# Attentions of the first block: steps of four heads instead of two, one step deep, with four fixed score banks

## The chip, the cores and the metric

The kernel runs on one core of one Trainium2 chip (trn2). The metric is the device time of one execution in microseconds. Five engines have queues of their own, each worked strictly in order: TensorE (PE; PEld is its weight loads), VectorE (DVE), ScalarE (ACT), GpSimd (POOL) and SyncE (SP), which here only issues DMAs. They meet at semaphores: an instruction waits until a counter has reached a value. TensorE writes to PSUM, which has eight banks of 512 fp32 columns by 128 partitions.

## The reference

Two transformer blocks of two layers each, one after the other, on 256 tokens of width 1024, in fp32. The change touches the first block alone, and in it the two attention branches of each layer. In layer 0 the 256 context tokens attend to themselves (256 keys) and the 256 tokens of x attend to both (512 keys); in layer 1 only the tokens of x do (512 keys).

```python
q_m = (rms_norm(c_q, lw["mla_q_g"]) @ lw["w_uq"]).reshape(B, S, MLA_HEADS, MLA_QK_DIM)
q_nope, q_rope = jnp.split(q_m, [MLA_NOPE_DIM], axis=-1)     # 64 and 32 wide, 8 heads
...
y_m = attend(q_m, k_m, v_m) @ lw["w_mo"]                     # scores = nope part + rope part
...
y_g = attend(q_g, k_g, v_g) @ lw["w_go"]                     # 8 query heads, 2 key heads, 64 wide
g_f, g_m, g_g = jnp.split(jax.nn.sigmoid(gate_logits + lw["b_gate"]), N_BRANCHES, axis=-1)
return (g_f * y_f + g_m * y_m + g_g * y_g) @ lw["w_o"]
```

`attend` is scores, softmax over the keys, product with the values. `y_f` is a two-dimensional Fourier transform of four groups of 128 features, times `w_fo`. The key of the rope part is one for all eight heads.

## The kernel before

Every weight matrix streams through a ring of four slots of 1 MB ("panels"). SyncE asks for panel n when TensorE has begun panel n-3. There are two kinds. An "a" panel (`w_ada`, the modulation) is used as it lands. A "d" panel is split first: ScalarE rounds it to fp32r (`split`, L2050), GpSimd forms the rest (L1995), and TensorE multiplies three times (high by high and low, then low by high). The order of both kinds is the string `RING`.

The heads of the first block lie in pairs: pair c has head a = 0 in partitions 0 to 63 and head a = 1 in 64 to 127. The rope parts have 32 rows per head; the two of pair c lie in the strips that begin at 32 (c % 2) and at 64 + 32 (c % 2), with four copies of the one rope key, one per strip.

**The attention loop.** `units(l)` lists units (kind m or g, context or x, pair c, query tile q of 128 queries): 32 in layer 0, 16 in layer 1. Loop step u does on TensorE, in order:

- the scores of unit u: one product of 64 rows per head into a bank each, and for kind m one more of 32 rows per head (L1316 on);
- the transposes of the probabilities of unit u-2 (`TURN`), a bank per head, 2 or 4 tiles of 128 keys each;
- whatever of the other work is listed for u: `modulate()` (GROUPS, two "a" panels, each 16 products of 256 columns in column strips of 32, and the transposes of the modulation before), a Fourier step (`dft_steps`: products with `dft_d`, one step later with `cos_s` and `nsin_s`), `dense(2)` (OPENED, a gate panel), and the products with `w_fo` (FOURIER);
- the value products of unit u-3 (`LAG`): one bank per pair, both query tiles in it.

ScalarE in its step: the copies of the turned probabilities to SBUF (L2303), the two exponentials (L2319), the copy of a modulation row (L2066), the even half of a Fourier result (L2337), two sigmoids (L2348), a rounding of one group of the Fourier branch in four steps from ROUND (L2355), and splits of panels in the steps of AHEAD. VectorE: two row maxima (L3210) and their scaling (L3214), reciprocal and scaling of the probabilities of the unit before (L3220, L3224), the sum of a modulation (L2832), the copy of an attention output every second step (L3191), the Fourier halves (L3198, L3201, L3252 to L3255), and the low parts (L3264).

**Banks.** Every result takes the next of the eight banks in turn (`Tally.take`, the same count in every engine's program). Before TensorE writes to a bank it waits until the result before in that bank has been read (`bank()`). `T.last()` is the last bank taken. The steps in which the other work stands are written out by hand in GROUPS, LAST, OPENED, FOURIER, ROUND and AHEAD, one entry per layer.

Of the kernel before, what the change touches and what calls it, by code (L numbers as in the profile page):

```python
# [35 lines left out]
P = 128  # L36
# [149 lines left out]
RING = "a" * (ADA_FIRST - EARLY_ADA) + "d" * 10 + "a" * 16 + "dddd" + "a" * 10 + "d" * 50 \  # L186
# [4 lines left out]
class Tally:  # L191
# [3 lines left out]
    def __init__(self):  # L195
        self.count = {}
        self.regs = []
        self.bank = 0
# [14 lines left out]
    def take(self):  # L213

        b = self.bank
        self.bank = (b + 1) % BANKS
        return b, self.next(f"bank{b}")

# [8 lines left out]
    def last(self):  # L227

        b = (self.bank - 1) % BANKS
        return b, self.value(f"bank{b}")  # L230
# [231 lines left out]
def units(l):  # L462

    return [(kind, half, c, q) for kind in "mg" for half in ((0, 1) if l == 0 else (1,)) for c in range(HEADS // 2)
            for q in range(2)]
# [16 lines left out]
def pv_opens(u, todo):  # L482

    return LAG <= u < len(todo) + LAG and todo[u - LAG][3] == 0


def build(nc, W, out, scratch, copies):
    with ExitStack() as ctx:
# [11 lines left out]
        prob, probT = area(PROB, 2, 2, TOK), area(PROBT, 2, 4, SEQ)  # L500
# [91 lines left out]
        def _(sp):  # L592
# [142 lines left out]
            def mix_and_mlp(l):  # L735
# [16 lines left out]
                modulations(*((8, 16) if l == 0 else (36, 8)))  # L752
                for n in (0, 512):
                    gates(0, n)
                modulations(*((24, 10) if l == 0 else (44, 2)))
# [139 lines left out]
        def _(pe):  # L895
# [415 lines left out]
            def attention(l, cols):  # L1311
                todo = units(l)
                n = cols.stop - cols.start
                pv = first = None
                turned = {}
# [5 lines left out]

                dense(2)
                pe.wait_ge(S["roped"], T.next("roped"))
                for u in range(len(todo) + LAG):

                    if u < len(todo):
                        kind, half, c, q = todo[u]
                        keys = slice(0, HALVES[half][1])
                        c0 = HALVES[half][0] + q * P
                        qs = slice(c0, c0 + P)  # L1330
                        bs = [bank() for _ in range(2)]
                        for a in range(2):
                            at = slice(HD * a, HD * a + HD)
                            x, y = (qn[at, c, qs], kn[at, c, keys]) if kind == "m" else (qg[at, c, qs], kg[at, keys])
                            mm = products(ps[:, bs[a], 0:keys.stop], [(x, y)], stop=kind == "g")
                            if kind == "g":
                                mm.then_inc(k.bank_done[bs[a]], 1)
                        if kind == "m":
                            for a in range(2):
                                r0 = HD * a + ROPE * (c % 2)  # L1340
                                rot = slice(r0, r0 + ROPE)
                                products(ps[:, bs[a], 0:keys.stop], [(qr[rot, (2 * c + a) // 4, qs], kr[rot, keys])],
                                         start=False).then_inc(k.bank_done[bs[a]], 1)
                    if TURN <= u < len(todo) + TURN:
                        _, half, _, _ = todo[u - TURN]
                        pe.wait_ge(S["prob_ready"], T.next("prob_ready"))
                        for a in range(2):
                            b = bank()
                            for t in range(HALVES[half][1] // P):
                                mm = flip(ps[:, b, t * P:t * P + P], prob[:, (u - TURN) % 2, a, t * P:t * P + P])  # L1350
                            mm.then_inc(k.bank_done[b], 1)
                        turned[u - TURN] = T.last()

                    if u in GROUPS[l]:
                        modulate()
                    if u == LAST[l]:
                        modulated_last()
                    if u == 0:
                        fin_in = dense(1)
# [28 lines left out]
                    if u >= LAG:  # L1388
                        kind, half, c, q = todo[u - LAG]
                        tt = HALVES[half][1] // P  # L1390
                        if pv_opens(u, todo):
                            pv = bank()
                        pe.wait_ge(*k.moved(turned[u - LAG]))
                        for t in range(tt):
                            for a in range(2):
                                at = slice(HD * a, HD * a + HD)
                                h = 2 * c + a
                                mm = products(ps[at, pv, q * P:q * P + P],
                                              [(vm[:, t, h * HD:h * HD + HD] if kind == "m" else vg[:, t, at],
                                                probT[:, (u - LAG) % 2, t, a * P:a * P + P])], t == 0, t == tt - 1)  # L1400
                        if q == 1:
                            mm.then_inc(k.bank_done[pv], 1)
# [618 lines left out]
        def _(act):  # L2021
# [258 lines left out]
            def attention(l, cols):  # L2280
# [10 lines left out]

                fin_tiles((1, 2))
                turned = {}
                for u in range(len(todo) + LAG):
                    if u < len(todo):
                        tiles = [T.take() for _ in range(2)]
                    if TURN <= u < len(todo) + TURN:
                        turned[u - TURN] = [T.take() for _ in range(2)]
                    if LAG <= u:
                        tt = HALVES[todo[u - LAG][1]][1] // P  # L2300
                        for a, (b, v) in enumerate(turned[u - LAG]):
                            act.wait_ge(k.bank_done[b], v)
                            act.activation(probT[:, (u - LAG) % 2, 0:tt, a * P:a * P + P],  # L2303
                                           ps[:, b, 0:tt * P].rearrange("p (t c) -> p t c", t=tt),
                                           ACT.Copy).then_inc(k.bank_read[b], 1)
                    if u in AHEAD[l] and u not in OPENED[l]:
                        split()
                    if u < len(todo):
                        kind, half, c, q = todo[u]
                        buf = u % 2  # L2310
                        n = HALVES[half][1]
                        tt = 2 * half + q
                        if u >= TURN:
                            b, v = turned[u - TURN][1]
                            act.wait_ge(k.bank_done[b], v)
# [8 lines left out]
                    if u in GROUPS[l]:  # L2324
                        modulate()
# [1560 lines left out]
```

## Time and profile before

| | us |
|---|---|
| three runs | 2749.25, 2754.78, 2753.53 |
| median | 2753.53 |
| span of the profiled execution | 2752.9 |
| TensorE busy in it | 2696.1 (98%) |
| stretch of the attention of layer 0 (149.20 to 367.42) | 218.22 |
| stretch of the attention of layer 1 (1017.93 to 1138.58) | 120.65 |

The span runs from the first to the last instruction; the median of the runs is 0.6 us above it. A matmul's own duration contains its way through the array, so durations of neighbours overlap; the distance between the starts of two groups, best seen at the weight loads (PEld), is what the first of them costs. Idle time of an engine stands in brackets, with what ended it.

### The profile page before, as it was taken

The page shows a single profiled execution, that of the slowest core. Times are in us where ns is not written, and L with a number is a line of the kernel's source. Part 1 is how long each engine was busy: PE and PEld are TensorE (multiplying, and loading weights), DVE is VectorE, ACT ScalarE, POOL GpSimd, SP SyncE. Part 2 cuts the span into 40 slices and gives each one's busy share as a digit, 9 for nine tenths or more (in the row PEclk, how much of TensorE's full clock was granted, in tenths as well). Part 3 has the DMA queues.
Part 4 walks back from the last instruction along what each step waited for, and adds up shares of the span by engine and source line. Part 5 has one row for each costly group of instructions (what it writes and reads, how often), then busy time and mean ns, then how long its engine had stood idle before and what let it go on. Part 6 is the DMA issues. An engine that isn't in the chain of part 4 may idle for free.

```text
span 2752.9 us, 43816 instructions
## 1 busy us (share of the span) xinstructions
PE 2696.1 (98%) x17615; PEld 2303.1 (84%) x17615; DVE 1019.1 (37%) x2146; ACT 1301.0 (47%) x1873; POOL 1766.3 (64%) x1446
## 2 busy tenths in 40 slices
PE   7999999999999999999999999999999999999998
PEld 5766588778888677898878899999899899989887
DVE  4253521441111544344345413454433413354441
ACT  4435622342222446645545544555545545554553
POOL 2503144434554243686987987559998997757997
PEclk9999999999999999999999999999999999999999
DMA  7554533323322254464545567435655558534554
GB/s 236 143 184 138 174 88 107 108 77 93 105 92 93 60 149 159 141 197 153 194 160 164 187 167 237 123 100 177 193 188 178 189 184 193 181 102 155 181 189 145
DMA packets 404056, 418.84 MB, mean 152 GB/s; under 512 B 80975, under 2 KB 373959, under 8 KB 403636
## 3 DMA queue, kind: packets, MB, share of 16 engines
q1 hardware_dynamic: 403892, 416.52, 49.1%
q8 instruction: 119, 1.95, 0.3%
q14 instruction: 45, 0.37, 0.0%
HBM read 415.42 MB, written 3.16 MB: 152 GB/s over the span
## 4 chain that ended last, share of the span: by engine, by line
PE 92%; DVE 3%; ACT 2%; POOL 1%; DMA 1%; issue 1%; SPq 0%; DVEq 0%; ACTq 0%; POOLq 0%
PE ps L960 21%; PE ps L944 18%; PE ps L928 16%; PE ps L1584 12%; PE ps L971 10%; PE ps L1592 6%; PE ps L988 2%; PE ps L1460 2%; PE ps L1485 2%; POOL ring_r L1995 1%; PE ps L1469 1%; PE ps L1491 1%; PE ps L1715 1%; DMA ring<-in_w_ada 1%; ACT ring_hi L2050 1%
## 5 line engine op out<-in xcount | busy, mean ns | idle before, releaser
L1995 POOL TENSOR_TENSOR ring_r<-ring,ring_hi 128x512 fp32r<-128x512 f32 (+1 forms) x1440 | 1763.8, 1262 | 969.5 <-ACT ring_hi L2050 943.9
L2050 ACT ACTIVATE ring_hi<-ring 128x2048 fp32r<-128x2048 f32 x312 | 597.0, 1914 | 234.2 <-DMA ring<-in_ffn_w_down 106.4
L960 PE MATMUL ps<-hT_r,ring_hi 128*128 128x256 f32 (+1 forms) x2816 | 468.0, 324 | 1.3 <-DVE arena L3676 1.2
L960 PEld LDWEIGHTS ps<-hT_r,ring_hi 128*128 128x128 f32 x2816 | 411.6, 191 | 51.5 <-issue 11.2
L1584 PE MATMUL ps<-hT_r,ring_hi 128*128 128x512 f32 x1408 | 339.3, 392 | 0.0
L1584 PEld LDWEIGHTS ps<-hT_r,ring_hi 128*128 128x128 f32 x1408 | 258.6, 188 | 53.2 <-issue 3.3
L944 PE MATMUL ps<-arena_r,ring_hi 128*128 128x256 f32 (+1 forms) x1712 | 291.0, 316 | 1.5 <-DVE arena_r L3315 1.5
L944 PEld LDWEIGHTS ps<-arena_r,ring_hi 128*128 128x128 f32 x1712 | 249.9, 190 | 22.4 <-DVE arena_r L3315 1.9
L971 PE MATMUL ps<-hT_r,ring_r 128*128 128x256 f32 (+1 forms) x1408 | 237.1, 321 | 0.0
L971 PEld LDWEIGHTS ps<-hT_r,ring_r 128*128 128x128 f32 x1408 | 207.2, 190 | 19.6
L928 PE MATMUL ps<-arena 128*64 128x128 f32 (+9 forms) x1616 | 183.6, 339 | 18.3 <-DVE arena L3191 9.6
L1592 PEld LDWEIGHTS ps<-hT_r,ring_r 128*128 128x128 f32 x1440 | 184.4, 191 | 6.9
L1592 PE MATMUL ps<-hT_r,ring_r 128*128 128x256 f32 x1440 | 186.7, 283 | 0.0
L928 PEld LDWEIGHTS ps<-arena 128*64 128x64 f32 (+4 forms) x1616 | 113.8, 159 | 60.7 <-issue 51.0
L944 PE MATMUL ps<-arena_r,ring_r 128*128 128x256 f32 (+1 forms) x856 | 159.8, 315 | 0.0
L960 PE MATMUL ps<-arena_r,ring_hi 128*128 128x256 f32 (+1 forms) x912 | 144.5, 311 | 0.9 <-POOL ring_r L1995 0.9
L944 PEld LDWEIGHTS ps<-arena_r,ring_r 128*128 128x128 f32 x856 | 129.6, 190 | 10.3
L960 PEld LDWEIGHTS ps<-arena_r,ring_hi 128*128 128x128 f32 x912 | 127.6, 189 | 12.4 <-issue 1.6
L2559 ACT ACTIVATE arena<-ps 128x256 f32<-128x256 f32 x176 | 58.0, 382 | 142.8 <-PE ps L1592 142.7
L3527 DVE TENSOR_TENSOR ps<-ps,arena 128x256 f32<-128x256 f32 x176 | 66.8, 424 | 155.8 <-ACT arena L2559 155.5
L3413 DVE TENSOR_TENSOR arena_r<-arena,arena_r 128x512 fp32r<-128x512 f32 (+1 forms) x64 | 54.5, 856 | 182.2 <-ACT arena_r L2464 182.1
L2464 ACT ACTIVATE arena_r<-arena 128x512 fp32r<-128x512 f32 (+1 forms) x64 | 33.3, 525 | 147.2 <-PE ps L944 106.3
(393 smaller groups left out, 3342.0 us busy)
## 6 DMA issues: line engine op xcount, KB each, us to landing
ring<-in_w_in SPq DMA_DIRECT2D x74, 1024.0 KB
ring<-in_w SPq DMA_DIRECT2D x64, 1024.0 KB
ring<-in_ffn_w_up SPq DMA_DIRECT2D x44, 1024.0 KB
ring<-in_ffn_w_gate SPq DMA_DIRECT2D x44, 1024.0 KB
ring<-in_ffn_w_down SPq DMA_DIRECT2D x44, 1024.0 KB
ring<-in_w_ada SPq DMA_DIRECT2D x40, 1024.0 KB
ring<-in_w_in SPq DMA_DIRECT2D x48, 256.0 KB
ring<-in_w_o SPq DMA_DIRECT2D x8, 1024.0 KB
```

The source lines that it names most:

```text
L928: mm = pe.matmul(o, lhsT, rhs, start=start and j == 0, stop=stop and j == len(passes) - 1, skip_group_check=True)
L944: last[t] = pe.matmul(o, lhsT, rhs, start=start and j == 0, stop=stop and j == n - 1, skip_group_check=True)
L960: mm = pe.matmul(o, w[0], a[x], start=j == 0 and x == 0, stop=False, skip_group_check=True)
L971: mm = pe.matmul(o, w[1], a[0], start=False, stop=j == len(tiles[0]) - 1, skip_group_check=True)
L988: return pe.transpose(o, src, ident)
L1460: mm = pe.matmul(ps[:, b, :].rearrange("p (x t) -> p x t", x=2), w[0][:, kt, m * P:m * P + P], k.h_both[:, kt, :, cols], start=kt == 0, st ...
L1584: mm = pe.matmul(ps[:, b, :].rearrange("p (x t) -> p x t", x=2), w[0][:, kt, m * P:m * P + P], k.h2_both[:, kt], start=kt == 0, stop=False ...
L1592: return [pe.matmul(ps[:, b, 0:SEQ], w[1][:, kt, m * P:m * P + P], h2[0][:, kt, :], start=False, stop=kt == KD - 1, skip_group_check=True) ...
L1995: ins = pool.tensor_tensor(k.ring_lo[s][:, part], k.ring[s][:, part], k.ring_hi[s][:, part], ALU.subtract)
L2050: act.activation(k.ring_hi[s][:, :], k.ring[s][:, :], ACT.Copy).then_inc(k.hi_ready[s], 1)
L2559: act.activation(low[:, m, :], ps[:, b, SEQ:2 * SEQ], ACT.Copy).then_inc(S["low_moved"], 1)
L3527: ins = dve.tensor_tensor(ps[:, b, 0:SEQ], ps[:, b, 0:SEQ], low[:, 2 * g + m, :], ALU.add)
```

## The change

A loop step now does four heads: two pairs c of the same query tile. Layer 0 has 16 steps and one closing step, layer 1 has 8 and one.

- TensorE begins step u with the transposes of the probabilities of step u-1 (16 or 8), then does the scores of step u: the 64-row parts of heads 0 and 1, then of heads 2 and 3, then for kind m the four rope parts, which lie in four different strips of 32 rows. Then the other work, and at the end the value products of step u-1 (32 or 16 instructions), which take one bank per step.
- The four scores have banks 4 to 7 for themselves. All other results rotate through banks 0 to 3 (`T.rotate(FEW)`), and through all eight again after the attention.
- ScalarE copies the turned probabilities first, then does four exponentials, then the other copies; the splits stand at the end of a step, after the sigmoids and the roundings. VectorE scales the probabilities of step u-1 first, then copies the attention output of step u-2, then does the maxima of step u.
- The probabilities have one buffer for four heads instead of two buffers for two.
- The four roundings of the Fourier branch, and their low parts, stand in one step (ROUND) instead of four.
- Two modulations stand in one step in steps 11 and 12 of layer 0; two "a" panels have moved behind the four gate panels in `RING`.
- In `branches` ScalarE's wait before a gate tile names the sum before it directly; it is the same wait, and the first group has none.

```diff
-RING = "a" * (ADA_FIRST - EARLY_ADA) + "d" * 10 + "a" * 16 + "dddd" + "a" * 10 + "d" * 50 \
+RING = "a" * (ADA_FIRST - EARLY_ADA) + "d" * 10 + "a" * 14 + "dddd" + "a" * 12 + "d" * 50 \
...
-        self.bank = (b + 1) % BANKS
+        self.bank = (b + 1) % self.rotating
...
-TURN, LAG = 2, 3
-GROUPS, LAST = ((1, 3, 5, 7, 9, 11, 12, 13, 19, 20, 22, 24, 26), (1, 3, 5, 7, 11)), (28, 13)
-OPENED = (15, 16, 17, 18), (7, 8, 9, 10)
-FOURIER = (32, 34), (16, 18)
-ROUND = 16, 8
-AHEAD = (13, 14, 15, 16, 29, 31, 32, 33), (6, 7, 8, 9, 14, 15, 16, 17)
+SCORE, FEW = 4, 4
+GROUPS, LAST = ((0, 1, 2, 3, 4, 5, 6, 11, 11, 12, 12, 13, 14), (0, 1, 2, 3, 7)), (15, 8)
+OPENED = (7, 8, 9, 10), (3, 4, 5, 6)
+FOURIER = (15, 16), (7, 8)
+ROUND = 10, 6
+AHEAD = (6, 7, 8, 9, 13, 14, 15, 16), (2, 3, 4, 5, 6, 7, 7, 8)
...
-    return {3 + j: u for j, u in enumerate(todo)}
+    return {1 + j: u for j, u in enumerate(todo)}
...
+def head_of(pair, j):
+
+    return 2 * pair + j // 2, j % 2, slice(HD * (j % 2), HD * (j % 2) + HD)
...
+                def scores(kind, half, pair, q):
+
+                    keys = slice(0, HALVES[half][1])
+                    qs = slice(HALVES[half][0] + q * P, HALVES[half][0] + q * P + P)
+                    bs = []
+                    for j in range(4):
+                        b, v = T.again(SCORE + j)
+                        pe.wait_ge(k.bank_read[b], v - 1)
+                        bs.append(b)
+                        c, a, at = head_of(pair, j)
+                        x, y = (qn[at, c, qs], kn[at, c, keys]) if kind == "m" else (qg[at, c, qs], kg[at, keys])
+                        mm = products(ps[:, b, 0:keys.stop], [(x, y)], stop=kind == "g")
+                        if kind == "g":
+                            mm.then_inc(k.bank_done[b], 1)
+                    for j in range(4 if kind == "m" else 0):
+                        r0 = HD * (j % 2) + ROPE * (j // 2)
+                        rot = slice(r0, r0 + ROPE)
+                        products(ps[:, bs[j], 0:keys.stop], [(qr[rot, pair, qs], kr[rot, keys])], start=False) \
+                            .then_inc(k.bank_done[bs[j]], 1)
+
+                def probabilities_turned(half):
+
+                    tt = HALVES[half][1] // P
+                    for j in range(4):
+                        if j % 2 == 0:
+                            pe.wait_ge(S["prob_ready"], T.next("prob_ready"))
+                        if j % (4 // tt) == 0:
+                            b = bank()
+                        for t in range(tt):
+                            o = (j * tt + t) % 4 * P
+                            mm = flip(ps[:, b, o:o + P], prob[:, j, t * P:t * P + P])
+                        if (j + 1) % (4 // tt) == 0:
+                            mm.then_inc(k.bank_done[b], 1)
+                    return T.last()
...
+                T.rotate(FEW)
+                for u in range(len(todo) + 1):
+
+                    if u > 0:
+                        turned = probabilities_turned(todo[u - 1][1])
                     if u < len(todo):
-                        kind, half, c, q = todo[u]
...
+                        scores(*todo[u])
+
+                    if u == 0:
+                        fin_in = dense(1)
+                    for _ in range(GROUPS[l].count(u)):
                         modulate()
...
-                    if u >= LAG:
...
+                    if u > 0:
+                        attended(*todo[u - 1], turned)
+                T.rotate(BANKS)
...
+                        for g in range(4):
+                            act.activation(branch_split[0][0][:, g, cols], fin[:, g, cols], ACT.Copy) \
+                                .then_inc(S["branch_rounded"], 1)
+                    for _ in range(AHEAD[l].count(u)):
+                        split()
...
+                for u in range(len(todo) + 1):
+                    if u > 0:
+                        probabilities(todo[u - 1][1])
+                    if u > 1:
+                        moved(*todo[u - 2])
                     if u < len(todo):
-                        maxima(u)
...
+                        maxima(*todo[u])
```

## Rows read from the trace of the kernel before

**Rows 1.** The page: busy time of the engines, and the chain that ended last.
```profile
PE 2696.1 (98%) x17615; PEld 2303.1 (84%) x17615; DVE 1019.1 (37%) x2146; ACT 1301.0 (47%) x1873; POOL 1766.3 (64%) x1446
...
PE 92%; DVE 3%; ACT 2%; POOL 1%; DMA 1%; issue 1%; SPq 0%; DVEq 0%; ACTq 0%; POOLq 0%
```
**Rows 2.** Windows: stretch, length, busy of each engine, clock, DMA share, GB/s.
```profile
149.20:367.42 218.22, 208.01 (x1646) 142.06 (x1645) 96.34 (x285) 113.14 (x245) 46.17 (x64) 1.00 0.50 160
...
1017.93:1138.58 120.65, 114.66 (x1021) 84.78 (x1021) 56.87 (x145) 75.95 (x135) 44.81 (x63) 1.00 0.47 149
```
**Rows 3.** TensorE's waits: total us, times, longest.
```profile
PE ps L928 <- DVE arena L3191: 9.6, 15, 0.7
```
**Rows 4.** Timeline of a step of layer 0, kind m, 512 keys: start, length, instruction.
```profile
213.51 0.30 PEld L928 LDWEIGHTS ps<-arena 64*128 64x128 f32 x4 [0.17 <-issue]
214.57 0.30 PEld L928 LDWEIGHTS ps<-arena 32*128 32x128 f32 x4 [0.76 <-issue]
215.62 0.85 PEld L988 LDWEIGHTS ps<-const,arena 128*128 128x128 f32 x8 [0.76 <-issue]
...
215.73 1.29 DVE L3210 TENSOR_REDUCE stat<-ps 128x1 f32<-128x512 f32 x2 [2.11 <-PE ps L928]
216.65 1.45 PEld L928 LDWEIGHTS ps<-ring,silu_c 128*32 128x32 f32 x32 [0.17 <-issue]
...
217.29 0.78 ACT L2319 ACTIVATE arena<-ps,stat,rstd 128x512 f32<-128x512 f32 x1 [3.45 <-DVE stat L3214]
...
218.51 0.42 PEld L988 LDWEIGHTS ps<-const,p_cmp 128*128 128x128 f32 x4 [0.41 <-issue]
...
218.82 0.59 ACT L2066 ACTIVATE hid_v<-ps 128x512 f32<-128x512 f32 x1
...
219.10 0.85 PEld L928 LDWEIGHTS ps<-arena 128*64 128x64 f32 x16 [0.17 <-issue]
...
219.29 1.09 ACT L2303 ACTIVATE arena<-ps 128x512 f32<-128x512 f32 x2
```
**Rows 5.** Timeline of a score group with 256 keys.
```profile
149.20 0.30 PEld L928 LDWEIGHTS ps<-arena 64*128 64x128 f32 x4 [0.35 <-issue]
...
149.83 0.30 PEld L928 LDWEIGHTS ps<-arena 32*128 32x128 f32 x4 [0.33 <-issue]
```
**Rows 6.** Timeline of a dense step of layer 0.
```profile
235.45 7.13 PEld L960 LDWEIGHTS ps<-hT_r,ring_hi 128*128 128x128 f32 x32
...
237.82 1.91 ACT L2050 ACTIVATE ring_hi<-ring 128x2048 fp32r<-128x2048 f32 x1
...
246.45 1.27 ACT L2348 ACTIVATE arena<-ps,vecT 128x512 f32<-128x512 f32 x2 [5.41 <-PE ps L971]
246.56 0.85 PEld L928 LDWEIGHTS ps<-arena 128*64 128x64 f32 x16 [0.35 <-issue]
```
**Rows 7.** Timeline of VectorE's Fourier pieces in layer 0.
```profile
205.93 0.29 DVE L3198 TENSOR_TENSOR arena<-arena,ps 128x127 f32<-128x127 f32 x1
...
206.46 0.42 DVE L3252 COPY arena<-ps 128x260 f32<-128x260 f32 x1
...
261.86 0.69 DVE L3264 TENSOR_TENSOR arena_r<-arena,arena_r 128x512 fp32r<-128x512 f32 x1
```
**Rows 8.** Timeline of two modulations close together in layer 0.
```profile
291.20 1.93 PE L928 MATMUL ps<-ring,silu_c 128*32 128x256 f32 x32
...
297.14 1.07 PE L928 MATMUL ps<-ring,silu_c 128*32 128x256 f32 x16 [0.16 <-DMA ring<-in_w_ada]
```
**Rows 9.** Window of 1 us beside them (last number: GB/s).
```profile
297.00:298.00 1.00, 0.86 (x16) 0.42 (x16) 0.59 (x2) 1.00 (x4) 0.00 (x0) 1.00 1.10 346
```
**Rows 10.** Timeline of TensorE near the start.
```profile
31.58 1.45 PE L928 MATMUL ps<-hT_r,ring_hi 128*128 128x512 f32 x4 [1.94 <-DVE hT_r L2948]
32.96 3.29 PE L928 MATMUL ps<-early,silu_c 128*32 128x256 f32 x32
```
**Rows 11.** Window of 1 us in it (clock: third number from the end).
```profile
33.00:34.00 1.00, 1.00 (x13) 0.54 (x16) 0.86 (x2) 0.33 (x1) 1.00 (x1) 0.50 1.10 347
```

More of the change, by code:

```diff
@@ new lines, in attended @@
+                def attended(kind, half, pair, q, turned):
+                    tt = HALVES[half][1] // P
+                    b = bank()
+                    pe.wait_ge(*k.moved(turned))
+                    for x in range(2):
+                        for t in range(tt):
+                            for a in range(2):
+                                c, _, at = head_of(pair, 2 * x + a)
+                                h = 2 * c + a
+                                mm = products(ps[at, b, x * P:x * P + P],
+                                              [(vm[:, t, h * HD:h * HD + HD] if kind == "m" else vg[:, t, at],
+                                                probT[:, (2 * x + a) * tt + t, :])], t == 0, t == tt - 1)
+                    mm.then_inc(k.bank_done[b], 1)
@@ new lines, in exponentials @@
+                def exponentials(kind, half, pair, q):
+                    n, tt = HALVES[half][1], 2 * half + q
+                    for j in range(4):
+                        b, v = T.again(SCORE + j)
+                        c, a, _ = head_of(pair, j)
+                        if j % 2 == 0:
+                            act.wait_ge(S["row_max"], T.next("row_max"))
+                        act.wait_ge(k.bank_done[b], v)
+                        act.activation(prob[:, j, 0:n], ps[:, b, 0:n], ACT.Exp, bias=k.stat[:, j:j + 1],
+                                       scale=rstd_cq[:, tt:tt + 1] if kind == "m" else rstd_qg[:, tt, c, a:a + 1],
+                                       accum_out=k.stat[:, 4 + j:5 + j]).then_inc(k.bank_read[b], 1)
@@ L3227, in attention, with maxima @@
[L3227 to L3235 removed]
+                def maxima(kind, half, pair, q):
+                    n, tt = HALVES[half][1], 2 * half + q
+                    score[:] = [T.again(SCORE + j) for j in range(4)]
+                    for x in range(2):
+                        two = score[2 * x:2 * x + 2]
+                        nmax = k.stat[:, 2 * x:2 * x + 2]
+                        for a, (b, v) in enumerate(two):
+                            dve.wait_ge(k.bank_done[b], v)
+                            ins = dve.tensor_reduce(nmax[:, a:a + 1], ps[:, b, 0:n], AX, ALU.max, negate=True)
+                        ins.then_inc(S["dve_step"], 1)
+                        dve.wait_ge(S["dve_step"], T.next("dve_step"))
+                        rstd = over(rstd_cq[:, tt:tt + 1], [P, 2]) if kind == "m" else rstd_qg[:, tt, 2 * pair + x, :]
+                        dve.tensor_tensor(nmax, nmax, rstd, ALU.mult).then_inc(S["row_max"], 1)
@@ new lines, in probabilities @@
+                def probabilities(half):
+                    n = HALVES[half][1]
+                    for x in range(2):
+                        rsum = k.stat[:, 4 + 2 * x:6 + 2 * x]
+                        dve.wait_ge(*k.moved(score[2 * x + 1]))
+                        dve.reciprocal(rsum, rsum).then_inc(S["dve_step"], 1)
+                        dve.wait_ge(S["dve_step"], T.next("dve_step"))
+                        for a in range(2):
+                            p = prob[:, 2 * x + a, 0:n]
+                            ins = dve.tensor_scalar(p, p, rsum[:, a:a + 1], None, ALU.mult)
+                        ins.then_inc(S["prob_ready"], 1)
```

185 lines of the change are left out of this document (47 added, 138 removed).

## The prediction

> **What bounds the kernel now.** I read the page first: TensorE is busy for 98% of the span and holds 92% of the chain that ended last, so time moves only if TensorE's own work or its waits move [rows 1]. Then the stretches: the change touches two, the attention of layer 0 (149.20 to 367.42, 218.22 us) and of layer 1 (1017.93 to 1138.58, 120.65 us); the other 2414 us stay as they are [rows 2]. Then TensorE's waits: the largest is 15 waits, 9.6 us, for VectorE's copy of an attention output (L3191) [rows 3], all in these stretches. The timeline prices single steps.
>
> **Prices.** Weight loads show when a group of products begins. A score pair (two heads, 512 keys) takes 1.06 us, its rope pair 1.05, eight transposes 1.03, a modulation group 1.86 before the next begins [rows 4]. With 256 keys a pair takes 0.63 [rows 5]. So 256 more keys cost 0.43 and the rest, 0.2, is a fixed part that each change of array shape costs; eight transposes stream 0.85 and pay 0.17. I take 0.17 per change, and 0.85 (0.43) as the stream of a pair. For the other engines: two maxima 1.29, two exponentials 0.77 each, two copies of turned probabilities 1.09, the copy of a modulation row 0.59 [rows 4]; a dense pair over 512 columns 11.1, its two sigmoids 1.27, a split 1.91 [rows 6]; VectorE's even/odd step 0.53 (to the start of the next row), the DFT copies about 0.8 after 0.42 of them, a low-part subtraction 0.69 [rows 7].
>
> **What goes.** Per four heads the rope parts stream once in four strips, not twice in two: 8 x 0.85 + 4 x 0.43 = 8.5 us (8 unit pairs with 512 keys over both layers, 4 with 256). This needs four strips abreast, which before never does; strips 0 and 64 do run abreast. Bounds: all of it, or none (0) if they run two and two. I take all, since the column-strip modulation shows 4 abreast: 32 products of 256 columns in 1.86 [rows 4] are 0.053 each, where a pair with 256 keys has 0.21 per pass. Writing out both orders, TensorE changes shape 206 times before and 128 after (one group of transposes, one of value products, two score pairs in a row): 78 x 0.17 = 13.3. The second score pair behind the first may pay 0.03 (my value) to 0.2: 24 x 0.03 = 0.7. Work removed: 8.5 + 13.3 - 0.7 = 21.1 us. The waits of before go too; 9.6 us for the output copy [rows 3] and smaller ones, which the walk below puts at 18.3 us together in the two stretches (busy time alone leaves 16.2 us idle, 10.2 and 6.0 [rows 2]).
>
> The Trainium skill (TensorE: Matmul & The Clock Gate, Part 3, measured speedup) has four row tiles of K=32 at 3.07x, not 4x. By that the rope group would stream 1.30 x 0.85, the work removed would be 2.5 us less, and my walk ends 2.4 us later. No row of before shows four row strips.
>
> **What comes.** Everything except the scores has four PSUM banks instead of eight, and a step is one deep. I wrote out the engines' queues and gave each piece its price above, 0.21 us from the end of a stream to its result and 0.09 per handover (the rope stream ends at 215.42, the maxima begin at 215.73 [rows 4]); the same walk of the kernel before gives 217.3 and 120.2 where the trace has 218.2 and 120.7, so it can be trusted to a microsecond or two on known pieces. Waits that it finds after (u is the new step):
> - Layer 0, u = 4 to 6 and layer 1, u = 2: the value products take the bank of the modulation, whose copy stands behind four exponentials. From the end of the scores: maxima and scaling to 1.8, four exponentials 3.1, copy 0.6, in all 5.5; TensorE is there at 4.0 (modulation 1.87, its transposes and 12 DFT products at about 0.11 each 2.0, change 0.17). 4 x 1.5 = 6.0.
> - Transposes at the head of a step wait for probabilities. VectorE does the even/odd step (behind ScalarE's small copy, behind the exponentials) and the DFT copies before it scales: 5.7 + 0.5 + 0.8 + 1.0 for the first pair = 8.1, TensorE is there at 7.4. Layer 0: 1.0, 1.6, 1.6, 1.7, 0.9, 0.9 at the heads of u = 2 to 7, and 0.6 to 0.9 at each of the four heads from u = 12 (2.7); layer 1: 1.3, 0.5, 0.9. In all 13.0.
> - Rounding of the Fourier branch, once in four steps, now stands whole in u = 10 (layer 0) and u = 6 (layer 1), behind the sigmoids of that step's dense tiles and ahead of VectorE's scaling. From the dense end: sigmoids 1.3, four roundings at 0.54, the last subtraction 0.7, scaling 0.7 to 1.0, against value products of 0.9 to 1.7: 4.7 and 2.5 us.
> - Two modulations in one step (u = 11, 12) take four panels of 1 MB. A panel asked for at 291.20 was used at 297.14, and DMA moves about 346 GB/s, 3.0 us per panel [rows 8, 9]; the fourth comes 2.2 to 2.6 us late. With 0.5 at u = 1: 5.6.
> - The first split for w_fo stands at the end of u = 13, and its panel is asked for only in u = 13. ScalarE waits for the landing, then splits (1.91), then copies the turned probabilities whose bank the modulation of u = 14 needs: 3.3.
> - Dense tiles for banks in layer 1 (u = 3) 1.7; small ones in both layers 1.6.
> Sum: 6.0 + 13.0 + 7.2 + 5.6 + 3.3 + 3.3 = 38.4.
>
> What hides the rest: ScalarE needs 2.2 (copies) + 3.1 + 0.6 + 0.2 in a step of 12.9 us, VectorE 7; in the dense steps 11 us of products cover both table loads, sigmoids and the split. Without them every step would wait like u = 6. The copy that caused the 15 waits still comes, but the transposes need its bank last of four, 1.3 us in.
>
> **Sum.** The stretches by the walk: layer 0 220.7 (before 217.3), layer 1 115.8 (before 120.2): +3.4 - 4.4 = -1.0 us, or by terms 38.4 - 18.3 - 21.1 = -1.0. One more term: in a long wait the clock can fall. At 33 to 34 us the granted clock is 0.50 (1.2 GHz) after a wait of 1.94 us, and a modulation that takes 1.93 [rows 8] took 3.29: +1.4 [rows 10, 11]. In both stretches it is 1.00 now [rows 2]. The new waits of 4.7 and 3.3 may each cost that; I count half a fall, +0.7. So -0.3: the profiled execution had a span of 2752.9, the runs a median of 2753.53 (0.6 more); I take 2753 us.
>
> **Rivals.**
> 1. No net change (forecast), 2753. For: two sides of about 39 us each, from rows.
> 2. Four rope strips run two and two. For: no row shows more than two row strips abreast, and each stream has its own PSUM bank. Against: column strips manage four. Place: the rope group of each of 12 steps, 1.9 us instead of 1.02 with 512 keys. Price: the walk with doubled streams ends 8.1 us later over both layers (some of it fills waits elsewhere), 2753 + 8 = 2761. It decides (slower by over 0.2%) from about 1.6 us for a rope group. The same sign, with less certainty: slower DMA (3.6 us per panel is +3.4) and two or three clock falls (+1.4 each).
> 3. The new waits are smaller than walked. The softmax chain is 5.9 us from the end of the scores by rows, but half of the 38 us come from the order of small pieces (modulation copy, even/odd, rounding) and from the landing of panels; if these overlap better and half the new waits are not there, 2753 - 19 = 2734; if a quarter, 2743. For: the walk puts every piece behind the one before it with a full latency of 0.09. Against: it hit the two known stretches.
> 4. It doesn't do what it says: if the second score pair paid 0.2, +3.4 us, 2756; inside the forecast.
>
> **Numbers.** Forecast 0.56, slower rival with its kin 0.22, faster rival 0.22. A change of 0.2% (5.5 us) is what a measurement here can tell. The forecast lies within 2748 to 2758.5 (terms 2 and 4 by halves, clock, DMA). The range takes the slower rival whole and the nearer part of the faster: 2742 to 2762. Faster 0.22, same 0.56, slower 0.22.
>
> **What would show it.** A rope group of about 1.0 us (0.6 with 256 keys) with eight loads; two score pairs in about 1.9; no wait for the output copy; layer 0 about 2.5 us longer, layer 1 about 4.5 us shorter; the longest waits at the transposes that follow the fourth gate tile pair of each layer, then at the second modulation of u = 11 and 12 and the first of u = 14. I am wrong if a stretch is off by more than 5 us, if rope groups take 1.6 us or more, or if the clock in the stretches falls below 0.97.

## The result, and the profile after

Over 17 runs of each kernel the time went from 2753.53 us (2749.25 to 2757.68) to 2759.58 us (2755.72 to 2766.66), a ratio of 1.0024 with a 95% interval of 1.0017 to 1.0031: 6 us slower. The forecast was no change, at 2753. The profiled execution below took 2762.6 us, 3 us above the median.

The page of the changed kernel: span, busy time, and the chain that ended last. They answer to [rows 1].

```profile
span 2760.8 us, 43791 instructions
...
PE 2683.1 (97%) x17615; PEld 2304.9 (83%) x17615; DVE 1019.7 (37%) x2146; ACT 1300.4 (47%) x1857; POOL 1767.9 (64%) x1446
...
PE 90%; DVE 4%; ACT 2%; DMA 2%; issue 1%; POOL 1%; SPq 0%; DVEq 0%; ACTq 0%; POOLq 0%
```

TensorE is busy 13 us less, and the span is 8 us longer: the time went into waits. The busy time is itself inflated, because products at half clock take up to twice as long, as shown further down. Windows of the two stretches, beside [rows 2] (the clock is the third number from the end):

```profile
149.43:381.45 232.02, 205.47 (x1645) 147.06 (x1645) 95.54 (x285) 112.09 (x229) 45.21 (x64) 0.94 0.47 150
1030.20:1146.39 116.19, 107.08 (x1020) 84.40 (x1020) 55.76 (x145) 75.82 (x135) 42.22 (x60) 1.00 0.48 155
```

Layer 1 takes 116.2 us, where the working had 115.8. Layer 0 takes 232.0, where it had 220.7; and its granted clock is 0.94, where before it was 1.00. The miss is in one stretch. TensorE's waits in the whole run (total, times, longest); the wait for the output copy of [rows 3] is not among them, which shows that the change did remove it:

```profile
PE ps L997 <- DVE arena L3247: 15.5, 15, 3.9
PE ps L937 <- DMA ring<-in_w_ada: 6.6, 5, 2.3
...
PE ps L937 <- ACT hid_v L2090: 4.3, 3, 1.4
PE ps L937 <- ACT arena L2336: 3.8, 1, 3.8
```

A step of layer 0 with 512 keys, weight loads of the timeline, beside [rows 4]; then one with 256 keys, beside [rows 5]:

```profile
186.98 0.30 PEld L937 LDWEIGHTS ps<-arena 64*128 64x128 f32 x4 [0.17 <-issue]
...
188.89 0.31 PEld L937 LDWEIGHTS ps<-arena 32*128 32x128 f32 x8 [0.76 <-issue]
189.97 1.45 PEld L937 LDWEIGHTS ps<-ring,silu_c 128*32 128x32 f32 x32 [0.76 <-issue]
...
149.43 0.73 PEld L937 LDWEIGHTS ps<-arena 64*128 64x128 f32 x8 [0.35 <-issue]
150.49 0.31 PEld L937 LDWEIGHTS ps<-arena 32*128 32x128 f32 x8 [0.33 <-issue]
151.13 0.99 PEld L969 LDWEIGHTS ps<-hT_r,ring_hi 128*128 128x128 f32 x5 [0.33 <-issue]
```

Two score pairs take 1.91 us and the four ropes 1.08, where two took 1.05; with 256 keys the ropes take 0.64. The four strips do run abreast.

Windows around the long waits of layer 0. In each group the first window holds the wait or its end, the second the low clock:

```profile
195.00:197.00 2.00, 1.09 (x16) 0.85 (x16) 1.42 (x7) 0.38 (x2) 0.00 (x0) 0.99 1.10 349
197.00:203.00 6.00, 5.11 (x20) 4.12 (x22) 2.12 (x6) 2.39 (x4) 0.00 (x0) 0.50 0.20 63
...
294.00:296.00 2.00, 0.00 (x0) 0.00 (x0) 1.66 (x3) 1.87 (x4) 0.00 (x0) 0.98 0.00 0
296.00:302.00 6.00, 4.38 (x24) 2.99 (x28) 3.74 (x14) 2.38 (x3) 0.00 (x0) 0.50 0.00 0
...
318.00:320.00 2.00, 1.07 (x16) 0.50 (x16) 0.00 (x0) 0.62 (x3) 0.00 (x0) 0.96 1.04 325
320.00:326.00 6.00, 4.98 (x37) 3.06 (x38) 1.75 (x7) 0.60 (x1) 0.00 (x0) 0.50 1.08 352
...
338.00:341.00 3.00, 0.26 (x2) 0.00 (x0) 2.24 (x6) 1.38 (x1) 0.00 (x0) 0.88 0.03 10
341.00:347.00 6.00, 4.93 (x40) 2.41 (x42) 0.19 (x1) 6.00 (x14) 5.39 (x8) 0.50 0.43 142
```

So there are four stretches at 1.2 GHz, of 6.8 us each when windows of 1 us are summed up. Below, a "fall" is such a stretch. Outside the two attention stretches the clock falls too, in about the same amount before and after the change (43 us at half clock in the profile of the kernel before, 40 in this one), so the difference lies in layer 0. What they cost is read from TensorE's timeline: the same group at either level.

```profile
195.26 1.09 PE L937 MATMUL ps<-arena 128*64 128x128 f32 x16 [1.43 <-ACT hid_v L2090]
197.89 3.68 PE L997 MATMUL ps<-const,arena 128*128 128x128 f32 x16 [1.54 <-DVE arena L3247]
...
213.53 2.08 PE L997 MATMUL ps<-const,arena 128*128 128x128 f32 x16 [0.67 <-DVE arena L3247]
...
297.62 1.97 PE L997 MATMUL ps<-const,arena 128*128 128x128 f32 x8 [3.88 <-DVE arena L3247]
301.53 2.51 PE L937 MATMUL ps<-ring,silu_c 128*32 128x256 f32 x32
...
307.92 1.07 PE L937 MATMUL ps<-ring,silu_c 128*32 128x256 f32 x16 [2.29 <-DMA ring<-in_w_ada]
...
318.23 1.07 PE L937 MATMUL ps<-ring,silu_c 128*32 128x256 f32 x16 [1.48 <-DMA ring<-in_w_ada]
321.02 1.93 PE L937 MATMUL ps<-ring,silu_c 128*32 128x256 f32 x16 [1.72 <-DMA ring<-in_w_ada]
...
342.07 3.64 PE L937 MATMUL ps<-ring,silu_c 128*32 128x256 f32 x32 [3.81 <-ACT arena L2336]
```

Sixteen transposes take 3.68 at 0.50 and 2.08 at 1.00, a modulation 3.64 instead of 1.93, half a modulation 1.93 instead of 1.07. The same subtraction over all groups in the four stretches gives 2.8, 2.4, 2.6 and 2.4 us, 10.2 in all. 220.7 + 10.2 = 230.9, against 232.0 measured. The first and third places have no single long wait: 1.43 and 1.54 us with 1.09 us of products between, and 1.48 and 1.72 with 1.07 between. Behind the wait of 2.29 us at 308 the clock did not fall (half a modulation in 1.07).

### The profile page after: what moved, and what is told of

It is laid out like the page before. It is cut to its first block, busy times and chain, and to the rows that moved or that the text cites. A ratio compares the mean times of both kernels' runs of the same rounds, so it can differ in the third digit from the quotient of the medians.

```text
span 2760.8 us, 43791 instructions
## 1 busy us (share of the span) xinstructions
PE 2683.1 (97%) x17615; PEld 2304.9 (83%) x17615; DVE 1019.7 (37%) x2146; ACT 1300.4 (47%) x1857; POOL 1767.9 (64%) x1446
## 4 chain that ended last, share of the span: by engine, by line
PE 90%; DVE 4%; ACT 2%; DMA 2%; issue 1%; POOL 1%; SPq 0%; DVEq 0%; ACTq 0%; POOLq 0%
PE ps L969 21%; PE ps L953 18%; PE ps L937 14%; PE ps L1608 12%; PE ps L980 10%; PE ps L1616 6%; PE ps L997 2%; PE ps L1484 2%; PE ps L1509 2%; DMA ring<-in_w_ada 1%; POOL ring_r L2019 1%; PE ps L1493 1%; PE ps L1515 1%; PE ps L1739 1%; ACT arena L2325 1%
## 5 line engine op out<-in xcount | busy, mean ns | idle before, releaser
L953 PEld LDWEIGHTS ps<-arena_r,ring_hi 128*128 128x128 f32 x1712 | 249.9, 190 | 22.4 <-DVE arena_r L3340 1.9
L937 PE MATMUL ps<-arena 128*64 128x128 f32 (+9 forms) x1616 | 165.5, 339 | 10.7 <-ACT hid_v L2090 4.3
```

Source lines behind the costliest of these rows:

```text
L937: mm = pe.matmul(o, lhsT, rhs, start=start and j == 0, stop=stop and j == len(passes) - 1, skip_group_check=True)
L953: last[t] = pe.matmul(o, lhsT, rhs, start=start and j == 0, stop=stop and j == n - 1, skip_group_check=True)
```

## The experiments

Theory A: the waits were walked rightly, and what came on top is the clock at half behind long waits in layer 0. Theory B: the low clock costs nothing that counts and the waits alone make the loss. "The walk" is the prediction's walk through the engines' queues, done again for each kernel. Each kernel has 4 to 12 timed runs beside 23 to 25 of the kernel before, whose median was 2751.2, 2751.1 and 2751.6 us in the three groups (the first of e1 to e4, the second of c1, e5, e6, the third of e7 to e9), so the ratios are compared; 0.001 is 2.75 us, and a difference of two of these ratios is known to about 0.0013 to 0.0020, 4 to 6 us. Stretches are from one profiled execution each, in us. The clock is the mean over the timed runs of the granted clock of the whole span. One execution isn't the mean: the profiled ones of e9, e8 and e1 were 8.4, 4.4 and 3.8 us faster than their medians.

```
kernel                      median    ratio [95%]               layer 0  layer 1  clock
before                      2753.53   1                         218.2    120.7    0.994
changed                     2759.58   1.0024 [1.0017, 1.0031]   232.0    116.2    0.990
c1 changed again            2757.55   1.0024 [1.0015, 1.0033]   228.2    116.6    0.990
e1 busy waits               2753.63   1.0010 [1.0001, 1.0019]   224.6    115.3    0.993
e2 low parts later          2751.15   1.0000 [0.9991, 1.0009]   222.9    114.2    0.991
e3 ropes two abreast        2760.65   1.0035 [1.0023, 1.0046]   228.9    117.8    0.991
e4 transposes behind        2738.95   0.9950 [0.9936, 0.9963]   215.1    112.1    0.991
e5 behind + low + spread    2721.56   0.9893 [0.9878, 0.9907]   199.4    113.5    0.995
e6 behind + ropes by two    2746.78   0.9984 [0.9976, 0.9993]   220.6    116.3    0.992
e7 seven idle waits         2752.45   1.0005 [0.9995, 1.0015]   215.4    122.7    0.989
e8 seven filled waits       2746.55   0.9978 [0.9969, 0.9988]   211.3    119.8    0.993
e9 in front + low + spread  2743.34   0.9972 [0.9962, 0.9982]   213.1    114.0    0.993
```

**c1: is the low clock an accident of one execution?**

> The changed kernel once more, beside the others of this group. The lengths of the stretches at half clock differ between executions (in the profiles so far 3.4 or 6.8 us each, also those of the kernel before, outside the attention). Theory A: the four places of layer 0 fall again (behind the waits of 1.4 and 1.5, 3.9, 1.5 and 1.7, 3.8 us), with lengths of 3.4 or 6.8 us each; layer 0 takes 226 to 232 us, the waits are those of the first profile within 0.3 us. Theory B (what came on top was an accident of one execution): no or one fall in layer 0, 221 to 223 us, and a time within 2 us of the kernel before.

Windows of its trace, the stretch of layer 0 and the four low places:

```profile
150.95:379.14 228.19, 202.43 (x1646) 146.02 (x1645) 95.71 (x285) 111.79 (x229) 45.15 (x64) 0.96 0.47 153
...
199.00:203.00 4.00, 3.73 (x18) 3.36 (x20) 1.50 (x5) 2.07 (x4) 0.00 (x0) 0.62 0.11 34
297.00:301.00 4.00, 3.51 (x16) 2.63 (x16) 1.87 (x8) 1.57 (x3) 0.00 (x0) 0.57 0.00 0
307.00:311.00 4.00, 3.75 (x34) 2.50 (x36) 1.08 (x6) 0.60 (x1) 0.00 (x0) 0.60 1.10 348
339.00:345.00 6.00, 5.59 (x46) 3.07 (x48) 0.76 (x4) 5.34 (x13) 5.47 (x8) 0.50 0.51 186
```

Four stretches again, three of them half as long (3.4 us), and one in another place: behind a panel wait of 2.52 us at 307 instead of the two at 318 and 321. The time is 6.6 us above the kernel before. Theory B's form of an accident is out; what differs between executions is the length and, in part, the place. TensorE's longest waits in layer 0 were the same to within 0.1 us, except for the panels (6.0 us in all instead of 6.6, longest 2.5) and the 3.8, which was 3.4; one wait in layer 1 was 1.9 instead of 1.6.

**e1: the same waits, with TensorE busy in them.**

```
 # probabilities_turned at the heads of u = 5 (3 products) and 11 (8), layer 0
+b = bank(); awake(b, busy)          # products into the bank that the transposes will fill
 pe.wait_ge(S["prob_ready"], ...)
 # second modulation of u = 12, ahead of each of its two panel waits: 3 such products
```

> Theory A: the walked waits of the changed kernel are right and what came on top are four stretches in layer 0 at a granted clock of 0.50, each behind a long wait of TensorE, worth 2.8, 2.4, 2.6 and 2.4 us. Theory B: the low clock is a by-product that costs nothing that counts; the waits are the loss. Here TensorE does products of no use inside three of these waits (3 at the head of u = 5, 8 at the head of u = 11, 3 and 3 in front of the two panels of the second modulation of u = 12, layer 0), into banks that it owns already. No wait gets shorter. A: the clock stays at 1.00 in the first three places and falls only behind the wait of 3.8 us in u = 14, which is left as it is; layer 0 takes 224 us instead of 232, the time is 2752 us. B: layer 0 stays at 232 (or grows by a piece of a product), 2759.6 us.

```profile
149.74:374.29 224.55, 205.25 (x1680) 147.95 (x1679) 95.81 (x285) 111.78 (x229) 45.25 (x64) 0.99 0.49 155
195.00:203.00 8.00, 7.51 (x54) 4.62 (x54) 3.55 (x12) 2.64 (x6) 0.00 (x0) 1.00 0.45 145
294.00:302.00 8.00, 6.71 (x73) 3.73 (x71) 4.15 (x16) 5.26 (x12) 0.00 (x0) 1.00 0.32 103
312.00:320.00 8.00, 6.97 (x69) 4.39 (x67) 1.84 (x8) 2.87 (x8) 0.00 (x0) 1.00 1.02 334
336.00:340.00 4.00, 4.00 (x42) 2.17 (x36) 0.36 (x2) 4.00 (x11) 4.00 (x7) 0.59 0.61 165
```

The clock is 1.00 in the three filled places and falls behind the wait of 3.64 us that was left idle. The second panel wait of u = 11 is left idle too, and the clock did not fall behind it:

```profile
303.58 1.07 PE L938 MATMUL ps<-ring,silu_c 128*32 128x256 f32 x16 [2.57 <-DMA ring<-in_w_ada]
```

Layer 0 takes 224.6 us (A said 224). In the timed runs the gain over c1 is 0.0014, 3.9 us, half of A's 7.8: A priced each fall at its length in the first profile, and c1 has three of half that length. The direction is A's; B's "no gain" lies outside, but only just. And of the three places only the second, the wait of 3.88 us, is one that fell in every profile that has it idle (the changed kernel, c1, e3). The first did not fall in e2 and e9 either, where its waits of 1.43 and 1.54 us are idle and at most 0.01 us different, and the third did not in c1, where it is a single wait of 1.74 us. For these two e1 alone proves little.

**e2: VectorE's low parts behind its scaling.** The wait of 3.9 us goes.

```
 if u > 1: moved(*todo[u - 2])
+if u == ROUND[l] + 1: (the four low parts)
 if u < len(todo): maxima(*todo[u])
...
-if u == ROUND[l]: (the four low parts)
```

> VectorE's four low parts of the Fourier branch move to the next step, behind its scaling of the probabilities and in front of the maxima. The wait of 3.9 us at the head of u = 11 goes, and 0.9 to 1.2 us in layer 1. Theory A (clock at half behind long waits): the second stretch at half clock goes too, layer 0 -7 us (4.7 by the walk and 2.4 of clock), layer 1 -1.2, 2751.5 us. Theory B (only the waits cost): layer 0 -4.7, layer 1 -1.2, 2753.7 us.

0.0024 less than c1, 6.6 us, between B's 5.9 and A's 8.1: this one doesn't tell them apart. Its timeline of TensorE:

```profile
199.12 2.08 PE L997 MATMUL ps<-const,arena 128*128 128x128 f32 x16 [1.54 <-DVE arena L3247]
...
300.32 1.93 PE L937 MATMUL ps<-ring,silu_c 128*32 128x256 f32 x16 [2.49 <-DMA ring<-in_w_ada]
...
313.93 1.93 PE L937 MATMUL ps<-ring,silu_c 128*32 128x256 f32 x16 [2.47 <-DMA ring<-in_w_ada]
```

The wait of 3.9 and its low clock are gone and the first place is at full speed, but behind the panel waits of 2.49 at 300 and 2.47 at 314 the clock falls, and again behind the 3.8: three falls of 3.4 us. It isn't that the fall at the wait of 3.9 kept the next one away: c1 and e3 have a fall behind 3.88 and another behind the panel wait of 2.45 to 2.52, and e1 has neither. Which panel wait falls differs between executions.

**e3: ropes two abreast, all else as changed.**

```
-for j in range(4): scores of head j
-for j in range(4 if kind == "m" else 0): rope part of head j
+for i in range(2):
+    for j in (2 * i, 2 * i + 1): scores of head j
+    for j in (2 * i, 2 * i + 1): rope part of head j     # kind m
```

> One part undone: score pair, its rope pair, score pair, its rope pair, as before the change, all else as changed. By rows the rope parts stream 12 more times (8 x 0.85 + 4 x 0.43 = 8.5 us) and 24 changes of shape of 0.17 come back (4.1), 12.6 us of work; but the first maxima and exponentials start 0.2 us earlier in each step, and the steps in which TensorE waits for the probabilities take much of the work into the wait: by the walk +1.8 us in layer 0 and +0.4 in layer 1, 2761.8 us. If the four strips abreast are worth their full work, 2772 us. Theory A adds: the waits get shorter by about 1 us a step, so a stretch at half clock may go (-2.8), 2759.

0.0011 more than c1, 3.0 us, where the working had 2.2; the noise of about 4 us leaves 0 possible and 12.6 not. So 12.6 us of TensorE work cost about 3. The traces show where it went. The waits for modulation copies, 8.1 us in c1 (L2090), are gone; those for the scaled probabilities are 15.7 us against 15.8; and a step with 512 keys, from the transposes at its head to the next ones, takes 11.97 us in e3 (187.60 to 199.57) and 12.23 in c1 (187.04 to 199.27). Its profile has three falls of 3.4 us, 7 us less at half clock than c1's, so about 2 us (7 at 0.3, an estimate) of the work's price may be hidden there. While the transposes at the head of the next step wait for the softmax of this one, a step is as long as that chain, and TensorE's work only fills it.

**e4: the transposes behind the scores, on TensorE alone.**

```
-if u > 0: turned = probabilities_turned(todo[u - 1][1])
 if u < len(todo): scores(*todo[u])
+if u > 0: turned = probabilities_turned(todo[u - 1][1])
```

> One part undone: on TensorE the scores of a step stand in front of the transposes of the last step's probabilities, on the other engines nothing moves. The scores need only the exponentials of the last step; the transposes then come 3 us later to probabilities that have been scaled for long. By the walk the 13.0 us of waits at the heads of the steps go and layer 0 ends 12.2 us earlier, layer 1 4.4. Theory A: with them go the stretches at half clock behind waits of 1.5 and 3.9 us (5.2 us), 2759.6 - 16.6 - 5.2 = 2738 us. Theory B: only the waits go, 2743 us.

The kernel gains 0.0074 on the changed one, 20.4 us (A: 21.8 at 2738 against 2759.6; B: 16.6; the noise of 4 us covers both), and beats the kernel before by 13.8. Layer 0 is 16.9 us shorter than in the first profile (12.2 by the walk; 17 us at half clock instead of 27, at 0.37 us each another 3.8) and layer 1 4.1 (4.4). TensorE's waits:

```profile
PE ps L937 <- DMA ring<-in_w_ada: 7.2, 6, 1.9
...
PE ps L997 <- DVE arena L3247: 5.5, 6, 2.8
PE ps L937 <- ACT arena L2336: 4.0, 2, 3.8
```

The 15 waits for the scaled probabilities, 15.5 us, are 6 and 5.5. What stays is the rounding (2.8), the doubled modulations' panels and the 3.8 behind the split.

**e6: four strips once more, where nothing swallows them.** e4 with e3's edit.

> On the kernel with the transposes behind the scores the ropes go back to two abreast behind each score pair. Theory A: four abreast is worth its full work where no wait follows; with the transposes in front the waits for the probabilities swallowed it. By rows 12.6 us of work come back, by the walk +7.1 us in layer 0 and +3.9 in layer 1, 2739 + 11 = 2750 us. Rival: the strips are worth little in any order (as the run with the transposes in front seemed to show, some 2 us), 2741 us.

0.0034 more than e4, 9.4 us (A 11, rival 2). The same edit costs 3.0 with the transposes in front and 9.4 behind; the difference of the two, 0.0023, is just clear of its noise of 0.0022, and the stretches of the profiles say the same (+1.9 us against c1, +9.7 against e4). The 12.6 us of work, four strips abreast and the changes of shape that they save, are worth three quarters of their price here; the order of the queue hid it.

**e5: e4 with e2's edit and layer 0's modulations spread.**

```
-RING = ... + "a" * 14 + "dddd" + "a" * 12 + ...
+RING = ... + "a" * 14 + "daadaadaad" + "a" * 6 + ...
-GROUPS[0] = 0, 1, 2, 3, 4, 5, 6, 11, 11, 12, 12, 13, 14
+GROUPS[0] = 0, 1, 2, 3, 4, 5, 6, 8, 9, 10, 11, 12, 13
 # the loads in the same order as RING
```

> On the kernel with the transposes behind the scores: VectorE's low parts a step later, and layer 0's modulations spread, one a step in u = 8 to 13 and none doubled, the panels ordered to match. By the walk layer 0 ends 7.3 us earlier than with the transposes behind alone, at 201 us, with no wait above 1.8 us, layer 1 stays at 112. Theory A: with the waits of 2.8, 1.8 to 1.9 and 3.8 us the last three stretches at half clock in layer 0 go (17 us at 0.50 in that profile, some 6 us), 2739 - 7 - 6 = 2726 us. Theory B: 2732 us.

```profile
150.22:349.65 199.43, 193.21 (x1646) 142.17 (x1645) 97.24 (x285) 110.03 (x229) 45.44 (x64) 1.00 0.54 175
999.54:1113.01 113.47, 107.80 (x1021) 85.98 (x1021) 55.40 (x145) 75.70 (x135) 44.92 (x64) 0.98 0.49 158
```

Layer 0 holds the clock at 1.00 throughout, and TensorE is idle in it for 6 us. The ratio is 0.9893, 29.4 us faster than the kernel before and 15.7 faster than e4 (A 13; B's 7 lies outside). Layer 1 is 1.3 us longer than in e4: its clock was 0.98, behind a wait of 1.98 us for POOL's low part.

**e9: the same two edits, transposes in front.**

> The changed kernel with its transposes in front, but with the low parts a step later and layer 0's modulations spread over u = 8 to 13. Only the long waits go: by the walk layer 0 ends 7.1 us earlier and layer 1 1.2, with waits of up to 1.6 us left. Theory A: the stretches at half clock behind the waits of 3.9, 2.5 and 3.8 us go too and only the first place (1.4 and 1.5 us) may fall, 2757.6 - 8.3 - 5 = 2744 us. Theory B: 2749 us.

0.0052 less than c1, 14.3 us (A 13.6; B's 8.6 lies outside). In the profiled execution layer 0 took 213.1 us at clock 1.00 (the walk had 213.6), although the waits of the first place and one of 2.27 us are still in it:

```profile
197.71 2.09 PE L999 MATMUL ps<-const,arena 128*128 128x128 f32 x16 [1.54 <-DVE arena L3249]
...
330.15 2.08 PE L999 MATMUL ps<-const,arena 128*128 128x128 f32 x16 [2.27 <-DVE arena L3249]
```

This execution was the fastest of the eight, with a clock of 0.996 against 0.9925 in the mean: the usual run has 41 us at half clock (twice the missing clock times the span) and e5's has 29. So a kernel with the transposes in front can hold the clock, but mostly doesn't hold it as well as e5; where it falls in the other runs no trace shows.

**e7 and e8: the clock's price by itself.** On e5, TensorE waits in seven steps after the scores until VectorE has the new maxima; e8 puts six products into each wait.

```
 scores(*todo[u]); maxed = T.next("row_max", 2)
 # u = 4, 6, 12, 14 of layer 0 and 2, 4, 6 of layer 1, ahead of the transposes:
+b = bank(); awake(b, EXTRA); pe.wait_ge(S["row_max"], maxed)      # EXTRA = 0 in e7, 6 in e8
```

> The clock's price by itself, first half of a pair. On the kernel with the transposes behind, the low parts later and the modulations spread, TensorE waits idle between scores and transposes until VectorE has the maxima of the new scores, in u = 4, 6, 12 and 14 of layer 0 and u = 2, 4 and 6 of layer 1 (512 keys each: 2.9 us from the end of the scores by rows, less where the step had a wait of 0.6 already). Nothing else waits longer, so the waits alone cost 7 x 2.9 - 1 = 19 us: 2721.6 + 19 = 2741 us. Theory A: an idle wait of this length drops the clock in most of the seven places, 3.4 or 6.8 us at 0.50 each, about 1.9 us on average, +13 us if all fall and +7 if every second: 2748 to 2754 us. Theory B (the clock costs nothing that counts): 2741 us, as the other half of the pair.

> The second half of the pair: the same seven waits, but TensorE does 6 products of no use (0.43 us each) in each. Both theories: 2741 us. Theory A: the granted clock stays at 1.00 in the seven places and the pair differs by 7 to 13 us; theory B: no difference in the pair beyond 2 us.

TensorE's timeline of e7 where it fell and where it didn't (a releaser "issue" stands for this wait):

```profile
187.57 1.06 PE L1000 MATMUL ps<-const,arena 128*128 128x128 f32 x8 [3.00 <-issue]
...
211.20 1.94 PE L1000 MATMUL ps<-const,arena 128*128 128x128 f32 x16 [3.00 <-issue]
...
305.97 1.94 PE L1000 MATMUL ps<-const,arena 128*128 128x128 f32 x8 [2.89 <-issue]
325.63 3.57 PE L1000 MATMUL ps<-const,arena 128*128 128x128 f32 x16 [2.16 <-issue]
```

At 187 and 211 the wait of 3.00 us left the clock at full speed (eight transposes in 1.06, sixteen in 1.94), at 306 and 326 shorter ones halved it; of the seven, three fell (the third at 1039, layer 1, behind 3.00 us), and one more fall lies behind a wait of 2.00 us for GpSimd at 1117. e8 has none in the two stretches. The pair differs by 0.0027, 7.4 us (5.9 between the medians), at the low edge of A's 7 to 13 and above B's 2. e8's median stands 5.6 us above the walked 2741, though its profiled execution took 2742.1. Most of that rest goes with the clock, 0.995 in the profile and 0.9931 in the mean (over e8's runs 0.001 goes with 2.1 us): in other runs it fell in places that no trace shows, and whether the filled waits are among them is open.

**The price.** Twice the missing clock times the span is the time at half clock: 54 to 58 us per run of the changed kernel (0.9902, 2755.7 and 0.9895, 2758), 34 to 37 before. The pair prices it at 0.27 us per us (the medians' 5.9 over 60.1 - 37.9; 0.33 by the ratios), the four places of the first profile at 0.37 (10.2 over 27.2). Some 20 us more at half clock are then 5 to 8 us. With the walked -1.0 that makes +4 to +7, and +6 was measured.

## Why the prediction was wrong

The step that failed is the last term of the sum: "I count half a fall, +0.7". It was mis-sized by a factor of about ten: four falls in each of the two profiles of the changed kernel, 10.2 us in the first and 5 to 8 on average (an estimate, from the price above). It failed in three ways.

- It took only the waits of 4.7 and 3.3 us as candidates. Both did fall (3.88 and 3.81 us measured). But the clock also fell behind two waits of 1.4 to 1.7 us with 1.1 us of products between, and in c1 behind a single one of 2.52. The prediction had these waits in its list (the modulation copy at 1.5 and the transposes behind it at 1.6; panels at 2.2 to 2.6) and priced them as waits alone.
- It took +1.4 for a fall from one modulation that was caught by it [rows 10]. A fall outlasts that group: in the first profile it went on for 6.8 us, and all that TensorE did in it took up to twice as long.
- It named the signal ("if the clock in the stretches falls below 0.97") as one that would prove it wrong, and put two or three falls among the kin of the slower rival. Four falls at its own +1.4 would have made the forecast 2758. The rows of before could not tell that four places would fall, since the clock stays at 1.00 in their stretches; but they could tell that the forecast hung on it.

The other steps, by name:

- Work removed, 21.1 us: busy time in layer 0 is inflated by the falls, but e9 and e5 do the same work at clock 1.00, in 195.0 and 193.2 us, against 208.0 [rows 2]; layer 1 has 107.1 against 114.7. Together 20.6 to 22.4. Right. The 128 changes of shape were 127 by the weight loads of the changed kernel.
- Four ropes abreast: 1.08 us a group against 1.02 predicted. Rival 2 (two and two, 1.9) is refuted by the trace, and e6 puts the gain at 9.4 us of time for 12.6 of work. By the Trainium skill (TensorE: Matmul & The Clock Gate, Part 3, Measured speedup vs the span model), which has 3.07x for four row tiles, a group would have taken 1.30 x 0.85 + 0.2 = 1.31, an estimate from that figure; the trace, with 1.08, doesn't agree.
- Second score pair at 0.03: 1.91 for two pairs is 0.85 + 0.85 + 0.2, right; rival 4 is out. (Its price by the same terms is 24 x 0.17 = 4.1, not 3.4. And 1.86 over 32 products is 0.058; the 0.053 has one change of shape taken off. Neither moves the forecast.)
- Waits for the modulation copy, 4 x 1.5: three in layer 0 and one in layer 1 at 1.43 each, right. Rounding, 4.7 and 2.5 at the head of u = 11 and of layer 1's u = 7: 3.88 and 1.68. Panels 5.6: 6.6. Split in u = 13, 3.3: 3.81. Waits at the transposes, 13.0 and with the rounding 20.2: 15.5 in all, a quarter less than walked; the walk as a whole stood up in layer 1 (116.2) and, at clock 1.00, in e9 (213.1 against 213.6).
- Layer 1: 115.8 predicted, 116.2. Rival 3, half or a quarter of the new waits missing, is out for the stretches as a whole: layer 1 and e9 came as walked.

That the total came to nearly nothing by the walk was right, and the runs show what the working didn't say: the removed work was worth little in this order, since most of it, when put back, fills waits (e3), and one swap of two groups in TensorE's queue gains 20 us on the changed kernel (e4).

## What to carry to other kernels

Price a new wait twice: its length, and the clock behind it. In the two stretches of these traces the clock fell behind all nine idle waits of 3.4 to 3.9 us, behind ten of seventeen of 2.1 to 3.0, and behind five of seven close pairs (1.4 to 1.5 us, then 1.5 to 1.9, with 1.1 us of products between); a us at half clock cost 0.27 to 0.37 us. So count a share of the falls, each with all that TensorE does in it and not with the next group alone, and don't trust one profile for how many there are.

When work is taken off the bounding engine, ask which wait the rest of the step ends in: if the engine's next instruction waits for this step's own result, the saving turns into waiting, and moving work that is ready in front of that instruction can be worth more than the saving.

## What the runs showed of the hardware

- The granted clock fell to 0.50 behind single waits of 2.0 to 3.9 us, and behind two of 1.4 to 1.9 us with 1.1 us of products between; of three waits of 3.00 us in one execution (e7) one fell and two didn't. The same wait may fall in one execution and not in the next (1.43 and 1.54 us: the changed kernel and c1 yes, e2 and e9 no), for 3.4 or for 6.8 us.
- A good part of the spread between runs of one kernel goes with this: over the 23 to 25 runs of the kernel before in each group a mean clock lower by 0.001 goes with 1.6 to 1.9 us more.
- Products of no use in a wait (0.47 us each, eight in 3.72 us in e1) were tried in ten places (three of e1, seven of e8, one profiled execution each), and the clock stayed at 1.00 in all. Idle, the same seven waits had three falls (e7).
- Four row strips of 32 rows stream in the time of two: the ropes of four heads take 1.08 us with 512 keys and 0.64 with 256, those of two heads in the kernel before 1.05 [rows 4] and 0.63 (149.83 to the next load at 150.46).
